# First mixer: the recurrence runs ahead of the attention, and half of the output product between the attention's steps

## The reference, cut to what matters

```python
def hybrid_mixer(x, w_in, ..., w_out):            # x: 1 x 256 x 1024
    proj = x @ w_in
    xr, yr, q, k, v, iq, ik, iw = jnp.split(proj, split_points, axis=-1)
    xr = causal_depthwise_conv(xr, conv_w, conv_b)
    rec = rg_lru(xr, ga_w, ga_b, gx_w, gx_b, lam) * jax.nn.gelu(yr)      # 256 x 512
    att = dsa_attention(q, k, v, iq, ik, iw)                             # 256 x 8 x 64
    mixed = jnp.concatenate([rec, att.reshape(bsz, s, 512)], axis=-1)
    return mixed @ w_out                                                 # 1024 x 1024

def rg_lru(x, w_a, b_a, w_x, b_x, lam):
    r, i = sigmoid(x @ w_a + b_a), sigmoid(x @ w_x + b_x)                # by blocks
    log_a = -LRU_C * r * softplus(-lam)
    a, u = exp(log_a), sqrt(-expm1(2.0 * log_a)) * (i * x)
    h_t = a_t * h_(t-1) + u_t                                            # a scan over time
```

## Time and profile before

| | us |
|---|---|
| median of 3 runs | 2681.74 (2680.95 to 2683.26) |
| the profiled execution | 2677.12 |
| its span | 2675.3 |
| TensorE matmul busy | 2249.4 (84%) |
| VectorE busy | 679.2 (25%) |
| ScalarE busy | 387.9 (14%) |
| GpSimd busy | 80.8 (3%) |
| attention of the first mixer, first logits to product | 86.09 to 117.49 |
| its output product | 28.71 |

### The profile page before, as it was taken

One profiled execution on the slowest core, in us unless ns is written; L12 is line 12 of the kernel. 1 busy time (PEld: TensorE's weight loads), 2 busy tenths in 40 slices (PEclk: granted clock), 3 DMA queues, 4 the chain that ended last, 5 costly groups with the idle time before them and its releaser, 6 DMA issues.

```text
span 2675.3 us, 28076 instructions
## 1 busy us (share of the span) xinstructions
PE 2249.4 (84%) x12302; PEld 1623.3 (61%) x12302; DVE 679.2 (25%) x1217; ACT 387.9 (14%) x754; POOL 80.8 (3%) x78
## 2 busy tenths in 40 slices
PE   8799998899999899999966665679999996566565
PEld 7688886578887789898522222248899862222221
DVE  3432203433211544322200000025443221000001
ACT  2310012241001411110200000022101010000001
POOL 1210000030000000000000000000000000000000
PEclk9899999999999899999977788889999998888887
DMA  5087723129752232327899999943322589999995
GB/s 218 31 311 294 274 79 128 67 80 361 275 216 84 84 125 79 120 101 269 339 409 409 409 409 409 409 181 128 111 69 90 187 349 408 409 409 409 409 409 229
DMA packets 196891, 654.50 MB, mean 245 GB/s; under 512 B 9512, under 2 KB 14504, under 8 KB 192296
## 3 DMA queue, kind: packets, MB, share of 16 engines
q1 hardware_dynamic: 196776, 652.80, 63.1%
HBM read 651.73 MB, written 1.05 MB: 244 GB/s over the span
## 4 chain that ended last, share of the span: by engine, by line
PE 65%; DMA 29%; DVE 3%; ACT 1%; SPq 1%; POOL 1%; issue 1%; POOLq 0%; DVEq 0%; ACTq 0%
PE bank L671 64%; DMA ring<-in_w_exp_up 7%; DMA PRGT<-in_w_exp_gate 6%; DMA PRGT<-in_w_exp_up 5%; DMA ring<-in_w_exp_gate 5%; DMA PRGT<-in_w_exp_down 5%; DMA ring<-in_w_exp_down 1%; SPq L617 1%; DVE stat L1549 1%; PE bank L1101 1%; DMA ring<-in_hy_w_in 0%; DVE sm L1690 0%; POOL PRGT L2708 0%; DVE R L1568 0%; ACT hT L2335 0%
## 5 line engine op out<-in xcount | busy, mean ns | idle before, releaser
L671 PE MATMUL bank<-hT,ring 128*128 128x256 f32 x3392 | 757.0, 383 | 10.3 <-ACT hT L2335 10.0
L671 PEld LDWEIGHTS bank<-hT,ring 128*128 128x128 f32 x3392 | 646.1, 192 | 107.5 <-issue 16.6
L671 PE MATMUL bank<-PRGT,ring 128*128 128x256 f32 (+4 forms) x1936 | 414.8, 376 | 3.9 <-ACT PRGT L2335 1.8
L671 PEld LDWEIGHTS bank<-PRGT,ring 128*128 128x128 f32 (+3 forms) x1936 | 353.1, 187 | 61.4 <-issue 5.7
L671 PE MATMUL bank<-PRGT,R 128*32 128x512 f32 x1120 | 170.5, 742 | 109.6 <-DMA PRGT<-in_w_exp_up 69.4
L671 PE MATMUL bank<-ring,R 128*32 128x512 f32 (+1 forms) x960 | 155.7, 761 | 116.0 <-DMA ring<-in_w_exp_up 61.9
L671 PEld LDWEIGHTS bank<-PRGT,R 128*32 128x32 f32 x1120 | 35.4, 124 | 236.4 <-issue 110.5
L671 PEld LDWEIGHTS bank<-ring,R 128*32 128x32 f32 (+1 forms) x960 | 34.6, 130 | 230.4 <-DMA ring<-in_w_exp_up 96.2
L671 PE MATMUL bank<-PRGT,SQ 128*32 128x512 f32 (+1 forms) x768 | 110.9, 652 | 70.9 <-DMA PRGT<-in_w_exp_down 59.4
L1733 DVE SCALAR_TENSOR_TENSOR PRGT<-PRGT,sm 128x3072 f32<-128x3072 f32 x28 | 95.7, 3418 | 221.6 <-DMA PRGT<-in_w_ada 221.6
L671 PEld LDWEIGHTS bank<-PRGT,SQ 128*32 128x32 f32 (+1 forms) x768 | 34.4, 134 | 134.1 <-DMA PRGT<-in_w_exp_down 83.8
(11 more groups left out here) (336 smaller groups left out, 1863.7 us busy)
## 6 DMA issues: line engine op xcount, KB each, us to landing
PRGT<-in_w_exp_down SPq DMA_DIRECT2D x40, 2048.0 KB, 24.0
PRGT<-in_w_exp_gate SPq DMA_DIRECT2D x36, 2048.0 KB, 23.8
PRGT<-in_w_exp_up SPq DMA_DIRECT2D x34, 2048.0 KB, 24.1
ring<-in_mlp_w SPq DMA_DIRECT2D x32, 2048.0 KB, 7.9
ring<-in_w_exp_up SPq DMA_DIRECT2D x30, 2048.0 KB, 24.3
ring<-in_w_exp_gate SPq DMA_DIRECT2D x28, 2048.0 KB, 24.3
PRGT<-in_w_ada SPq DMA_DIRECT2D x32, 1536.0 KB, 10.8
ring<-in_w_exp_down SPq DMA_DIRECT2D x24, 2048.0 KB, 23.9
```

Source lines behind the costliest of these rows:

```text
L671: return mm(o, lhsT=lhsT, rhs=rhs, start=first, stop=last, **kw)
```

## The change

VectorE does all four parts of the recurrence ahead of the attention; the wait for the gelu's sigmoid moves behind the scans. On ScalarE that sigmoid moves ahead of the copy of the query's second bank. On TensorE the product's half for the recurrence's tiles is taken out of `lin_out`: for output banks 2 and 3 it is made behind the first three logits, in `acc[2]` and `acc[3]`; ScalarE copies these to `R[:, 4:8]`, and VectorE adds the scaled residual to them there. For output banks 0 and 1 it is made behind outputs 1 and 2, in their own banks, which stay open. At the end the half for the attention's tiles is added to banks 0 and 1, and made afresh for banks 2 and 3, to which VectorE adds `R`.

```diff
@@ -846,7 +846,7 @@
             for m in (BANK_AT["hy_q"], BANK_AT["hy_q"] + 1):
                 pe.wait_ge(bank_read[m % BANKS], filled(m))
 
-            def attention(name, pairs, done, q, k, v):
+            def attention(name, pairs, done, q, k, v, ahead=None, beside=None):
 
                 n0 = BANK_AT[name]
 
@@ -872,6 +872,8 @@
                     o = acc[2 + hp % 2]
                     if done + hp >= 2:
                         pe.wait_ge(sems["att_read"], done + hp - 1)
+                    elif ahead:
+                        pe.wait_ge(sems["part_read"], hp + 1)
                     for h in range(2):
                         pe.wait_ge(sems["probs_read"], 2 * (done + hp) + h + 1)
                         hs = slice(64 * h, 64 * h + 64)
@@ -881,19 +883,54 @@
 
                 for hp in range(3):
                     logits(hp)
+                if ahead:
+                    ahead()
                 for hp in range(pairs):
                     turn(hp)
                     if hp + 3 < pairs:
                         logits(hp + 3)
                     output(hp)
+                    if beside:
+                        beside(hp)
 
             pe.wait_ge(sems["inputs_loaded"], 32)
 
             def lin_out(name, done, pairs):
                 pe.wait_ge(sems["att_read"], done + pairs)
-                if done == 0:
-                    pe.wait_ge(sems["rec_done"], 1)
                 lin8(name, lambda k: MIX[:, k, :])
+
+            def hy_out_half(j, o, tiles, fresh):
+
+                s, u = SLOT_AT["hy_out"][j // 2]
+                pe.wait_ge(slot_full[s], loaded(u))
+                W = slot(s, KT)
+                c0 = 2 * (j % 2)
+                for h in range(2):
+                    for k in tiles:
+                        ins = mul(o[:, h * S:(h + 1) * S], W[:, k, (c0 + h) * P:(c0 + h + 1) * P], MIX[:, k, :],
+                                  fresh and h == 0 and k == tiles[0], False, skip_group_check=True)
+                return ins
+
+            REC, ATT = range(4), range(4, 8)
+
+            def rec_parts():
+                pe.wait_ge(sems["rec_done"], 1)
+                for j in (2, 3):
+                    hy_out_half(j, acc[j], REC, True).then_inc(sems["part_full"], 1)
+
+            def rec_held(hp):
+                if hp in (1, 2):
+                    n = BANK_AT["hy_out"] + hp - 1
+                    pe.wait_ge(bank_read[n % BANKS], emptied(n))
+                    hy_out_half(hp - 1, bk(n), REC, True)
+
+            def hy_out_rest():
+                pe.wait_ge(sems["att_read"], 4)
+                for j in range(4):
+                    n = BANK_AT["hy_out"] + j
+                    if j >= 2:
+                        pe.wait_ge(bank_read[n % BANKS], emptied(n))
+                    hy_out_half(j, bk(n), ATT, j >= 2).then_inc(bank_full[n % BANKS], 1)
 
             def ffn_and_ple(l, mixer):
 
@@ -962,8 +999,8 @@
 
             pe.wait_ge(bank_read[(BANK_AT["dsa_v"]) % BANKS], filled(BANK_AT["dsa_v"]))
             attention("dsa", 4, 0, lambda hp, h, tt: PR[64 * h:64 * h + 64, Q0 + hp, tt * P:(tt + 1) * P],
-                      lambda hp, h: PR[64 * h:64 * h + 64, KD, :], lambda hp, h, kt: vi(kt, 0, 64))
-            lin_out("hy_out", 0, 4)
+                      lambda hp, h: PR[64 * h:64 * h + 64, KD, :], lambda hp, h, kt: vi(kt, 0, 64), rec_parts, rec_held)
+            hy_out_rest()
             ffn_and_ple(0, "hy_out")
 
 
@@ -1657,10 +1694,10 @@
                     v.tensor_scalar(den, den, 2.0, -1.0, ALU.mult, ALU.add).then_inc(sems["vec_chain"], 1)
                     dve.wait_ge(sems["vec_chain"], L.up())
                 if part == 2:
-                    dve.wait_ge(sems["gelu_sig"], L.nxt("gelu_sig"))
                     for c in range(4):
                         v.tensor_tensor_scan(PR[:, XC + c, :], R[:, 4 + c, :], PR[:, IG + c, :], 0.0, ALU.mult, ALU.add).then_inc(sems["vec_chain"], 1)
                         dve.wait_ge(sems["vec_chain"], L.up())
+                    dve.wait_ge(sems["gelu_sig"], L.nxt("gelu_sig"))
                     v.tensor_tensor(z, z, xc, ALU.mult).then_inc(sems["vec_chain"], 1)
                     dve.wait_ge(sems["vec_chain"], L.up())
                 if part == 3:
@@ -1698,22 +1735,31 @@
                     v.reciprocal(sm[:, RS + p_:RS + p_ + 4], sm[:, RS + p_:RS + p_ + 4]).then_inc(sems["dsa_sum"], 1)
 
                 if slopes:
-                    recurrence(0)
+                    for part in range(4):
+                        recurrence(part)
                 masked_max(0)
                 for hp in range(pairs):
                     if hp + 1 < pairs:
                         masked_max(hp + 1)
                     inverse_sum(hp)
-                    if slopes and hp:
-                        recurrence(hp)
+                    if slopes and hp == 2:
+                        dve.wait_ge(sems["part_read"], 2)
+                        r_ = flat(R[:, 4:8, :])
+                        v.scalar_tensor_tensor(r_, flat(xT[:, 4:8, :]), ALPHA, r_, ALU.mult, ALU.add).then_inc(sems["vec_chain"], 1)
+                        dve.wait_ge(sems["vec_chain"], L.up())
 
             def out_and_norm(name):
 
                 for j in range(4):
                     n = BANK_AT[name] + j
                     dve.wait_ge(bank_full[n % BANKS], filled(n))
-                    v.scalar_tensor_tensor(R[:, 2 * j:2 * j + 2, :], xT[:, 2 * j:2 * j + 2, :], ALPHA, two(bk(n)[:, :]),
-                                                ALU.mult, ALU.add).then_inc(bank_read[n % BANKS], 1)
+                    if name == "hy_out" and j >= 2:
+                        r_ = flat(R[:, 2 * j:2 * j + 2, :])
+                        ins = v.tensor_tensor(r_, r_, bk(n)[:, :], ALU.add)
+                    else:
+                        ins = v.scalar_tensor_tensor(R[:, 2 * j:2 * j + 2, :], xT[:, 2 * j:2 * j + 2, :], ALPHA, two(bk(n)[:, :]),
+                                                     ALU.mult, ALU.add)
+                    ins.then_inc(bank_read[n % BANKS], 1)
                 for m in range(BANK_AT[name], BANK_AT[name] + 4):
                     dve.wait_ge(bank_read[m % BANKS], filled(m))
                 layer_norm()
@@ -2401,11 +2447,11 @@
             copy_out(BANK_AT["hy_yr1"], flat(PR[:, YR + 2:YR + 4, :]))
             act.wait_ge(sems["decay_den"], 1)
             f(th, th, ACT.Sqrt).then_inc(sems["decay_sqrt"], 1)
-            for j in range(2):
-                copy_out(BANK_AT["hy_q"] + j, flat(PR[:, Q0 + 2 * j:Q0 + 2 * j + 2, :]))
+            copy_out(BANK_AT["hy_q"], flat(PR[:, Q0:Q0 + 2, :]))
             z = flat(R[:, 0:4, :])
             act.wait_ge(sems["gelu_in"], L.nxt("gelu_in"))
             f(z, z, ACT.Sigmoid, scale=2 * math.sqrt(2 / math.pi)).then_inc(sems["gelu_sig"], 1)
+            copy_out(BANK_AT["hy_q"] + 1, flat(PR[:, Q0 + 2:Q0 + 4, :]))
 
             def attention(pairs, done, scale, mix0):
 
@@ -2433,6 +2479,10 @@
                 for hp in range(pairs):
                     if hp + 1 < pairs:
                         exponents(hp + 1)
+                    if done == 0 and hp == 0:
+                        for j in range(2):
+                            act.wait_ge(sems["part_full"], j + 1)
+                            f(flat(R[:, 4 + 2 * j:6 + 2 * j, :]), acc[2 + j][:, :], ACT.Copy).then_inc(sems["part_read"], 1)
                     turned(hp)
                     if hp:
                         output(hp - 1)
```

More of the change, by code:

```diff
@@ L329, in build @@
             "inputs_loaded", "x_loaded", "p_loaded", "small_loaded", "pos_loaded",
-            "lam_abs", "lam_log", "lam_ready", "conv_taps", "conv_done", "rg_input", "decay_tanh", "decay_den", "decay_sqrt", "gelu_in", "gelu_sig", "rec_done",
+            "lam_abs", "lam_log", "lam_ready", "conv_taps", "conv_done", "rg_input", "decay_tanh", "decay_den", "decay_sqrt", "gelu_in", "gelu_sig", "rec_done", "part_full", "part_read",
             "dsa_max", "dsa_exp", "dsa_sum", "dsa_probs", "probs_turned", "probs_read", "att_full", "att_read",
```

## The result

The changed kernel takes 2660.91 us in the median (2660.34 to 2661.29) against 2681.34 for the kernel before: a ratio of 0.9926, 95% interval 0.9914 to 0.9939. That is 20.4 us faster. The direction and the mechanism held; the amount didn't.

What follows compares the result with a forecast made beforehand. VectorE's softmax and recurrence chain, then TensorE's output product, were taken to bound the stretch to 146.20 us. Gain 16.8 - 0.2 - 1.1 = 15.5 us, from a median of 2681.74 to 2666.2; range 2662.7 to 2673.2.

Steps and rivals of the forecast that it cites:

- Which stage, which end: Attention and output product: the product's end, 146.20 us, is the quantity to forecast; everything behind it moves with it.
- Part 1: Recurrence ahead of the attention on VectorE: 10.3 us of work ending at about 85.1, costing nothing ahead of 87 us.
- Part 2: Half of the output product between attention steps: product's end from 146.2 to 129.4, 16.8 us less at full clock.
- early half: 32 product records behind the first three logits, in TensorE's idle stretch: 89.8 to 96.8 us, 6.96 us long.
- held blocks: 16 product records behind each of outputs 1 and 2, 3.48 us each, done at 106.6 and 112.6.
- The allowance for the clock: Attention steps: 1.1 us taken off the gain for one spell at the lower clock over a block of product records.
- GpSimd's sums: Sums of banks at the product's end, finishing about when the last bank is full: 0.2 us taken off, bounds 0 and 1.
- The clock rival: Attention steps and the product blocks between them stay at half clock: gain 4 to 12 us, middle 2673.7; chance 0.16.
- moves by the same amount: Whole kernel: the median, 4.6 us above the profiled execution, shifts equally with it, from 2681.74 to 2666.2 us.
- The recurrence in time: Rival ahead of the attention: VectorE's moved work ends past 87.1, gain about 14.5 or 11 us; chance 0.07 beyond the range.
- Slower: Remaining half of the product also at half clock, ending at 154.8, 8.6 us later: 2690 us; chance 0.03.
- not what it says: Behind the first logits: an unseen wait makes the 32 records run late, gain 3 to 6 us, 2677; chance 0.04.

Runs made afterwards that it cites:

- the early half alone: The changed kernel without the product blocks behind outputs 1 and 2; banks 0 and 1 made whole at the end: 2665.22 us, ratio 0.9947 to before.
- The filler: Kernel before with the recurrence moved ahead, plus 32 throw-away matmul records behind the first logits, product whole at the end: 2670.98 us, ratio 0.9970.
- the recurrence alone: Kernel before with only VectorE's recurrence and ScalarE's gelu sigmoid moved as in the change, TensorE's order unchanged: 2670.69 us, ratio 0.9971.

## Why the prediction was right and where it was wrong

**Which stage, which end: right.** The MLP's loads are issued at 129.10, 0.1 us behind the product's end, as before at 146.30, and all of the change's certain gain lies in the stretch.

**Part 1: right in effect, its slack mis-sized.** The recurrence ends at 86.19, not 85.1. The scaled product that I took at 1.52 us took 3.26 beside GpSimd's gelu product, and that took 3.20 (2.35 before). The times look like taking turns: GpSimd's ends at 78.95, and VectorE's 1.08 us later, where a product of this size with GpSimd idle takes 1.2. The scaling and the scans were shorter than their rows of before, 0.69 for 1.41 and 2.87 for 3.72, with GpSimd idle beside them. The moved work took 11.0 us from its start (75.20) to its end against 10.3, and the 2.0 us of slack shrank to 1.15. The Trainium skill ("VectorE: DVE Perf Modes", section "Two Vector instructions with no wait between them") has an operation with two SBUF tensors read one of them through an interface that GpSimd shares. The trace agrees that they get in each other's way, and has the price, which that section does not give: VectorE's product is 1.7 us over my 1.52, GpSimd's 0.85 over its 2.35.

**Part 2: the ledger held, step by step.** With the 0.32 us by which this execution reached its first logits later: early half 90.0 to 97.0 (forecast 89.8 to 96.8), held blocks done at 106.2 and 112.1 (106.6 and 112.6), the rest from 114.93 (115.5), the end at 129.0 (129.4). Net of the offset it is 0.7 us better: GpSimd's second probabilities took 1.6 us where I put 1.93 to 2.5, and outputs took 0.9 to 1.2 where I put 1.5. Idle time between the first logits and the product is 28.53 - 25.75 = 2.8 us (some 2 forecast). The stretch gave 17.5 us, where 15.5 were forecast: 0.7 from here and 1.3 from the allowance below. (One number of the prediction is misread: what leaves the tail is 28.71 - 13.92 = 14.8 us, not 13.8; the 16.8 does not use it.)

**The allowance for the clock: wrong.** I took off 1.1 us for one spell at the lower clock and 0.2 for GpSimd's sums. The clock is 1.00 in all of the stretch, and the sums ended 0.1 us before the product. So this term should have been nothing. In the spans the other 0.7 us are lost again: the changed kernel's trace came to its first logits 0.3 us later and took 0.4 longer behind. The clock rival (0.16) had its place in kernels that I hadn't forecast: with the early half alone the clock falls at pair 2. My reason for the full clock, though, was half wrong. The filler shows that a full clock at the entry is not enough and buys nothing where the steps wait for other engines; in the change it is the dense blocks between the steps that hold it. They are not the only way: the recurrence alone has the full clock in pairs 2 and 3 without any block, behind a wait of 1.63 us, while it fell behind waits of 2.37 (filler) and 3.26 us (early half alone).

**The step that put the time outside the range: "moves by the same amount".** I set the median 4.6 us above the profiled execution in both kernels. The trace of before was a lucky execution. Against the medians of the seven traces it is 1.6 us early ahead of the stretch (86.09, 87.7) and 2.3 short behind it (2529.3, 2531.6), and against the mean 0.6 short in the stretch (59.95, 60.6): together 4.5 of the 4.6. The change's own profiled execution is only 0.6 us under its median. So of the 20.4 us, 17.5 are the stretch in the trace that I had, 0.6 the scatter of the stretch that the change removes, and 2.3 are left over, ahead and behind. There the medians of the traces differ by 1.4 us (87.7 and 86.3) and 2.0 (2531.6 and 2529.6). The first comes mostly from a product that precedes the change, the second mostly from the 16 records of two lengths. No run shows that the second belongs to the change, and none excludes it. The comparison itself can't tell: its interval of 0.9914 to 0.9939 is 16.4 to 23.1 us, and the stretch's 18.1 lies in it. I had taken a lucky sample for a fixed distance, and had given only 0.02 to a gain above 18.5. With 0.6 us in place of 4.6 the forecast would have been 2662.2, outside my range and 1.3 us over the measured 2660.9.

**The other rivals.** The recurrence in time: yes, by 1.15 us. Slower, and not what it says: nothing of either showed.

## What to carry to other kernels

Lay out the queue of the engine that will be the bound, step by step, with what releases each step; it gave every landmark here within 0.9 us, the later start of the execution taken out. But check first how far executions of the kernel before scatter around the one that was traced, and put that scatter into the range. A change that fills idle gaps of TensorE also removes the scatter in them, which was worth 0.6 us in the mean here; the largest part of the miss, 2.3 us, lies in stages that the change does not touch. Fill gaps with work that has to be done anyway, and spread it over the gaps: in the stretch, half at the entry alone or half between the steps alone gave 4.7 and 1.55 us, both 9.7.

## What the runs showed of the hardware that I had not expected

- The same program has different clocks in different executions, and lengths that go with them: the stretch of before 59.9 or 61.5 us, 16 records far behind it 3.69 or 6.1. The first product takes 14.58 to 16.57 us, which looks like the same, though its PEclk is 1.00. The Trainium skill ("TensorE: Matmul & The Clock Gate", section "What's actually happening") says that how many matmuls run at the low clock varies from run to run of one kernel; the traces agree. Where TensorE is dense (the stretch of the change), six traces agree to 0.01 us.
- Records with one row of weights let the clock fall although TensorE is busy: 0.63 against 1.00 in the window with 128 rows of zeros, 8 us in the kernel.
- VectorE and GpSimd hold each other up on operations that read SBUF. A VectorE product of 128x1024 took 1.22 us with GpSimd idle, 1.52 beside its probabilities and 3.26 beside its gelu product; the scaling 0.69 with GpSimd idle and 1.41 beside the probabilities; four scans 2.87 and 3.72. The longest product ended 1.1 us, and the longer scaling 0.55 us, behind the end of the GpSimd operation beside it. An operation that VectorE had begun 0.16 us before GpSimd's kept its 1.20 us.
